# Layer 0's modulation in two halves, part of it multiplied on TensorE, and three half units ahead of it; products of a unit ordered by operand

## The reference

```python
c_act = jax.nn.silu(c)
for i in range(DEPTH):
    mod = c_act @ ada_w[i] + ada_b[i]
    sh1, sc1, g1, sh2, sc2, g2 = jnp.split(mod[:, None, :], 6, axis=-1)
    h = rms_norm(x, norm_mix[i]) * (1.0 + sc1) + sh1
    y = dilated_attention(h, ...)     # layer 0; hgrn2_mixer in layer 1
    x = x + g1 * y
    h = rms_norm(x, norm_ffn[i]) * (1.0 + sc2) + sh2
    x = x + g2 * swiglu(h, ffn_w1[i], ffn_w3[i], ffn_w2[i])
```

## Time and profile before

| | |
|---|---|
| median of 3 runs | 886.82 us (885.11 to 888.82) |
| the profiled execution's own time | 887.45 us |
| its span in the profile | 885.4 us |
| TensorE busy | 835.9 us, 94% of the span |
| VectorE busy | 613.0 us, 69% |
| ScalarE busy | 428.2 us, 48% |
| GpSimd busy | 125.0 us, 14% |
| data moved | 188.96 MB, mean 213 GB/s |

### The profile page before, as it was taken

One profiled execution on the slowest core, in us unless ns is written; L12 is line 12 of the kernel. 1 busy time (PEld: TensorE's weight loads), 2 busy tenths in 40 slices (PEclk: granted clock), 3 DMA queues, 4 the chain that ended last, 5 costly groups with the idle time before them and its releaser, 6 DMA issues.

```text
span 885.4 us, 10784 instructions
## 1 busy us (share of the span) xinstructions
PE 835.9 (94%) x4195; PEld 702.6 (79%) x4195; DVE 613.0 (69%) x736; ACT 428.2 (48%) x532; POOL 125.0 (14%) x160
## 2 busy tenths in 40 slices
PE   1599999999999989999999988999999899999998
PEld 0477888887888877888888877888888688888886
DVE  5979787788787856667756765787767665654554
ACT  3255454455455646344334355768475553433431
POOL 4101010101110100001010000376630000000000
PEclk9999999999999999999999999999999999999999
DMA  9899787877886823688787744443343477765621
GB/s 338 295 300 322 265 272 245 270 244 240 266 252 239 268 96 122 218 269 280 264 283 261 246 159 143 151 135 105 135 143 106 150 250 237 236 211 188 190 95 47
DMA packets 120039, 188.96 MB, mean 213 GB/s; under 512 B 5628, under 2 KB 91062, under 8 KB 119990
## 3 DMA queue, kind: packets, MB, share of 16 engines
q1 hardware_dynamic: 105782, 137.90, 48.2%
q0 software_dynamic: 14208, 50.39, 16.6%
HBM read 187.18 MB, written 1.09 MB: 213 GB/s over the span
## 4 chain that ended last, share of the span: by engine, by line
PE 85%; DVE 5%; DMA 3%; ACT 3%; issue 2%; SPq 2%; DVEq 0%; ACTq 0%
PE bank L454 71%; PE bank L756 3%; PE bank L588 2%; PE bank L563 2%; DMA raw<-in_attn_w_qkv_dram 1%; PE bank L544 1%; DVE acc L1198 1%; PE bank L509 1%; PE bank L707 1%; ACT arena L879 1%; DMA arena<-in_distance_table_dram 1%; DMA bias_rows<-arena 1%; SPq L303 1%; PE bank L506 1%; DVE acc L1193 1%
## 5 line engine op out<-in xcount | busy, mean ns | idle before, releaser
L1173 DVE TENSOR_TENSOR wlo<-raw,whi 128x2048 fp32r<-128x2048 f32 x123 | 285.4, 2324 | 50.8 <-ACT whi L830 50.7
L454 PE MATMUL bank<-whi,hT_hi 128*128 128x512 f32 (+1 forms) x776 | 305.1, 393 | 10.3 <-DVE hT_lo L1265 7.2
L454 PE MATMUL bank<-wlo,hT_hi 128*128 128x512 f32 (+1 forms) x800 | 306.2, 383 | 0.0
L454 PE MATMUL bank<-whi,hT_lo 128*128 128x512 f32 (+1 forms) x776 | 297.1, 383 | 0.0
L830 ACT ACTIVATE whi<-raw 128x2048 fp32r<-128x2048 f32 x123 | 235.4, 1916 | 34.2 <-DMA raw<-in_attn_w_qkv_dram 27.9
L454 PEld LDWEIGHTS bank<-whi,hT_hi 128*128 128x128 f32 x776 | 147.0, 189 | 41.2 <-DVE hT_lo L1265 9.4
L454 PEld LDWEIGHTS bank<-wlo,hT_hi 128*128 128x128 f32 x800 | 151.4, 189 | 29.1 <-issue 1.7
L454 PEld LDWEIGHTS bank<-whi,hT_lo 128*128 128x128 f32 x776 | 146.6, 189 | 28.9
L351 POOL DMA_DIRECT2D ada_w<-in_ada_w_dram x80 | 42.7, 534 | 523.9 <-DVE acc L1198 523.9
L1198 DVE SCALAR_TENSOR_TENSOR acc<-ada_w,cact,acc 128x1024 f32<-128x1024 f32 x80 | 102.3, 1279 | 3.0 <-DMA ada_w<-in_ada_w_dram 1.7
L454 PE MATMUL bank<-whi,oT_hi 128*128 128x512 f32 x240 | 97.2, 405 | 0.0
(11 more groups left out here) (146 smaller groups left out, 775.6 us busy)
## 6 DMA issues: line engine op xcount, KB each, us to landing
raw<-in_ffn_w_dram SPq DMA_DIRECT2D x88, 512.0 KB, 4.9
ada_w<-in_ada_w_dram POOLq DMA_DIRECT2D x80, 512.0 KB, 5.0
raw<-in_attn_w_qkv_dram SPq DMA_DIRECT2D x64, 512.0 KB, 5.7
raw<-in_ffn_w_dram SPq DMA_DIRECT2D x22, 1024.0 KB, 4.9
raw<-in_hgrn_w_in_dram SPq DMA_DIRECT2D x16, 1024.0 KB, 5.4
arena<-in_ada_w_dram POOLq DMA_DIRECT2D x16, 512.0 KB, 6.5
raw<-in_attn_w_qkv_dram SPq DMA_DIRECT2D x4, 1024.0 KB, 6.4
raw<-in_attn_w_out_dram SPq DMA_DIRECT2D x4, 1024.0 KB, 6.0
```

The costliest lines, as they stand in the source:

```text
L454: mm = nc.tensor.matmul(d[:, 0:n], l, r[:, k, cut], start=first and k == 0 and q == 0, stop=last and k == nk - 1 and q == 2)
L1173: nc.vector.tensor_tensor(wlo[:, m % RAW, :], raw[:, m % RAW, :], fp(hi_of(m)), ALU.subtract).then_inc(s["split"], 1)
```

## The change

The shift and the scale of layer 0 are worked out by halves instead of by blocks: half 0 is columns 0 to 511 of both shift and scale, half 1 the columns 512 to 1023 of both (`halves`). A chunk is still 128 rows and 512 KB, now in two pieces. Half 0 serves k-tiles 0 to 3, half 1 k-tiles 4 to 7.

- All these chunks, x, and the weight units go through SyncE's queue alone, in an order written out: c, chunks 0 and 1, x, chunks 2 to 7, unit 0 in four parts, chunk 8, unit 1, chunks 9 to 12, unit 2, chunks 13 to 15, then units from 3 on. The small rows, the relative bias and the distance table go through GpSimd's queue. The eight buffers are at other places, so that units can be loaded while they are in use.
- Of half 0's eight chunks VectorE adds up three (0, 2, 4); five (1, 3, 5, 6, 7: `ON_PE`) are multiplied by TensorE, eight one-column products each with the chunk as the stationary operand (`first_product`). Half 1 is all VectorE's (`first_sum`). The bias of the modulation comes in by its own rows.
- The raw transposed x is copied out of PSUM by ScalarE, and scale and shift are applied in place in SBUF.
- The order of the first head pair's units is changed (`ORDER0`): the three first are the upper halves (k-tiles 0 to 3) of chunks 0, 1 and 2, in three pairs of banks; units 3 to 5 are the lower halves. In these three (`first_half`) the products with `whi` come first for both tiles, then those with `wlo`.
- In every unit the products are ordered by operand: for a token tile all hi with whi, then all hi with wlo, then all lo with whi. The first waits for `rounded` and the hi part of the activation alone, `split` and the lo part are waited for where they are read.
- Later modulation blocks begin at unit 6 and take 8/5 products a unit in place of 11/8.

```diff
+ORDER0 = (0, 2, 4, 1, 3, 5, 6, 7, 8)
+ON_PE = (1, 3, 5, 6, 7)
...
+                j = ORDER0[j] if pr == 0 else j
...
-                if m == 0:
-                    sp.wait_ge(s["ada_used"], KC)
-                if PREFETCH <= m < RAW:
-                    sp.wait_ge(s["split"], m - PREFETCH + 1)
...
+            def first_load(n):
+                blk, k = divmod(n, KC)
+                if blk and k in ON_PE:
+                    sp.wait_ge(s["first_mm"], ON_PE.index(k) + 1)
+                elif blk:
+                    sp.wait_ge(s["first_sum"], first_sums(0, k) + 1)
+                sp.dma_start(first_w[k].rearrange("p (w c) -> p w c", w=2),
+                             halves(a["ada_w"][0, k * P:(k + 1) * P, :], blk)).then_inc(first_in[n], 16)
+            def load_unit(m):
                 if m >= RAW:
                     sp.wait_ge(s["pe_unit"], m - RAW + 1)
+                for src, nk, c0, n in pieces(m):
+                    slot = raw[:, m % RAW, :].rearrange("p (k n) -> p k n", k=nk)
+                    sp.dma_start(slot[:, :, c0:c0 + n], src).then_inc(raw_in[m % RAW], 16)
+            sp.dma_start(rows[0:KC, :], a["c"].rearrange("a (k d) -> (a k) d", d=P)).then_inc(s["c_in"], 16)
+            for n in range(2):
+                first_load(n)
+            sp.dma_start(x[:], a["x"][0].rearrange("(t p) d -> p t d", p=P)).then_inc(s["x_in"], 16)
+            for n in range(2, KC):
+                first_load(n)
+            for k in range(0, 4, 2):
+                for src, nk, c0, n in pieces(0):
+                    slot = raw[:, 0, :].rearrange("p (k n) -> p k n", k=nk)
+                    sp.dma_start(slot[:, k:k + 2, c0:c0 + n], src[:, k:k + 2, :]
+                                 ).then_inc(raw_in[0] if k else s["half_in"], 16)
+            first_load(KC)
+            load_unit(1)
+            for n in range(KC + 1, KC + 5):
+                first_load(n)
+            load_unit(2)
+            for n in range(KC + 5, 2 * KC):
+                first_load(n)
+            for m in range(3, UNITS):
...
+                if n == 2 * KC:
+                    pool.wait_ge(s["first_sum"], first_sums(1, KC))
                 if n >= 2 * KC + ADA_RING:
-                    pool.wait_ge(s["ada_used"], n - ADA_RING + 1)
+                    pool.wait_ge(s["ada_used"], n - 2 * KC - ADA_RING + 1)
...
+                def product(lhs, w, t, start, stop):
+                    for k in ks or range(nk):
+                        for c in cols or range(len(dst[t])):
+                            mm = nc.tensor.matmul(dst[t][c][:, 0:n], lhs[:, k0 + k, t * P:(t + 1) * P],
+                                                  w[:, k, c * 512:c * 512 + n],
+                                                  start=start and k == 0, stop=stop and k == nk - 1)
+                    return mm
+
+                pe.wait_ge(s["rounded"], m + 1)
+                for name, value in high:
+                    pe.wait_ge(s[name], value)
                 for t in tiles:
-                    for k in ks or range(nk):
-                        hi = lhs_hi[:, k0 + k, t * P:(t + 1) * P]
-                        lo = lhs_lo[:, k0 + k, t * P:(t + 1) * P]
-                        for c in cols or range(len(dst[t])):
-                            d = dst[t][c]
-                            cut = slice(c * 512, c * 512 + n)
-                            for q, (l, r) in enumerate(((hi, w[0]), (hi, w[1]), (lo, w[0]))):
-                                mm = nc.tensor.matmul(d[:, 0:n], l, r[:, k, cut],
-                                                      start=first and k == 0 and q == 0,
-                                                      stop=last and k == nk - 1 and q == 2)
+                    product(lhs_hi, w[0], t, first, False)
+                    if t == tiles[0]:
+                        pe.wait_ge(s["split"], m + 1)
+                    product(lhs_hi, w[1], t, False, False)
+                    if t == tiles[0]:
+                        for name, value in low:
+                            pe.wait_ge(s[name], value)
+                    mm = product(lhs_lo, w[0], t, False, last)
...
-                        pe.wait_ge(s["xn_lo"], 4 * q + 2 * t + j + 1)
-                        unit(m + j, hT_hi, hT_lo, 4, 4 * j, 512, dst, j == 0, j == 1, tiles=(t,))
-                    if q == 0:
-                        continue
+                        n = 4 * q + 2 * t + j + 1
+                        unit(m + j, hT_hi, hT_lo, 4, 4 * j, 512, dst, j == 0, j == 1, tiles=(t,),
+                             high=[("xn_hi", n)], low=[("xn_lo", n)])
...
+            def first_product(k):
+                pe.wait_ge(first_in[k], 16)
+                slot = ON_PE.index(k)
+                for j in range(KC):
+                    mm = nc.tensor.matmul(bank[3][:, slot * KC + j:slot * KC + j + 1], first_w[k][:, j * P:(j + 1) * P],
+                                          cact[:, k:k + 1], start=True, stop=True)
+                mm.then_inc(s["first_mm"], 1)
+            def first_reduce(half, dst):
+                pe.wait_ge(s["first_sum"], first_sums(half, KC))
+                for j in range(KC):
+                    mm = nc.tensor.matmul(dst[:, j:j + 1], acc[:, half, j * P:(j + 1) * P], ones[:, 0:1],
+                                          start=True, stop=True)
+                mm.then_inc(s["mod_red"], 1)
+            pe.wait_ge(s["c_in"], 16)
             pe.wait_ge(s["pool_setup"], 5)
-            nc.tensor.transpose(bank[0][:, 0:NROWS], rows[0:NROWS, :], ident[0:NROWS, 0:NROWS]).then_inc(s["cols_t"], 1)
+            nc.tensor.transpose(bank[0][:, 0:KC], rows[0:KC, :], ident[0:KC, 0:KC]).then_inc(s["c_t"], 1)
+            pe.wait_ge(s["cact_s"], 1)
+            first_product(1)
+            first_product(3)
+            pe.wait_ge(s["rows_in"], 16 * (len(ROWS) + 1))
+            nc.tensor.transpose(bank[1][:, 0:NROWS], rows[0:NROWS, :], ident[0:NROWS, 0:NROWS]).then_inc(s["cols_t"], 1)
+            norm_t(0, 0)
+            first_product(5)
+            norm_t(0, 1)
             pe.wait_ge(s["rel_in"], 16 * 5)
-            nc.tensor.matmul(bank[1][0:GH, 0:TABLE], rel3, tabw, start=True, stop=True).then_inc(s["tab_mm"], 1)
-            for t in range(T):
-                norm_t(0, t)
-            for r in range(3):
-                reduce_task(r, 3 if r < 2 else 2)
+            nc.tensor.matmul(bank[2][0:GH, 0:TABLE], rel3, tabw, start=True, stop=True).then_inc(s["tab_mm"], 1)
+            first_reduce(0, bank[3][:, len(ON_PE) * KC:(len(ON_PE) + 1) * KC])
+            first_product(6)
+            first_product(7)
...
+            def first_half(m):
...
+                if m == 0:
+                    pe.wait_ge(s["half_rounded"], 1)
+                    pe.wait_ge(s["xn_hi"], 1)
+                    product(hT_hi, w[0], 0, True, False, ks=(0, 1))
+                    pe.wait_ge(s["rounded"], 1)
+                    product(hT_hi, w[0], 0, False, False, ks=(2, 3))
+                else:
+                    pe.wait_ge(s["rounded"], m + 1)
+                    product(hT_hi, w[0], 0, True, False)
+                pe.wait_ge(s["xn_lo"], 1)
+                product(hT_lo, w[0], 0, False, False)
+                pe.wait_ge(s["xn_hi"], 2)
+                product(hT_hi, w[0], 1, True, False)
+                pe.wait_ge(s["xn_lo"], 2)
+                product(hT_lo, w[0], 1, False, False)
+                if m == 2:
+                    first_reduce(1, bank[7])
+                pe.wait_ge(s["split"], m + 1)
+                product(hT_hi, w[1], 0, False, False)
+                product(hT_hi, w[1], 1, False, False).then_inc(s["pe_unit"], 1)
+            first_half(0)
             pe.wait_ge(s["tab_cp"], 1)
+            pe.wait_ge(s["mod_sum"], 1)
+            first_half(1)
+            pe.wait_ge(s["h0_raw"], 4)
+            first_half(2)
...
+            def first_modulation(half):
+                dve.wait_ge(s["mod_red"], half + 1)
+                src = bank[7][:, 0:KC]
+                if half == 0:
+                    dve.wait_ge(s["first_mm"], len(ON_PE))
+                    src = small[:, 48:56]
+                    n = (len(ON_PE) + 1) * KC
+                    nc.vector.tensor_reduce(src, bank[3][:, 0:n].rearrange("p (s j) -> p j s", j=KC), AX_X, ALU.add
+                                            ).then_inc(s["mod_sum"], 1)
+                    dve.wait_ge(s["mod_sum"], 1)
+                at = 48 if half else 56
+                b = cols[:, BIAS0:BIAS0 + 2 * KC].rearrange("p (w h c) -> p w h c", w=2, h=2)[:, :, half, :]
+                v = lambda y: y.rearrange("p (w c) -> p w c", w=2)
+                nc.vector.tensor_tensor(v(small[:, at:at + KC]), v(src), b, ALU.add).then_inc(s["mod_sum"], 1)
+                dve.wait_ge(s["mod_sum"], half + 2)
+                scale_gain(0, 0, small[:, at + 4:at + 8], 4 * half, 4).then_inc(s["mod_ev"], 1)
+                dve.wait_ge(s["mod_ev"], half + 1)
...
+            first_sum(0, 4)
```

(25 more changed lines are left out.)

363 lines of the change are left out of this document (204 added, 159 removed).

## The result

| | before | changed |
|---|---|---|
| median of 20 runs | 887.88 us (884.07 to 891.51) | 890.17 us (884.68 to 893.52) |
| ratio | | 1.0027, 95% interval 1.0014 to 1.0039 |
| the profiled execution's time, span | 887.45, 885.4 | 889.58, 887.8 |

The changed kernel is 2.3 us slower. That is less than 0.5%, yet the interval leaves no doubt of the sign. The forecast was 883.0 with a range up to 888: the time lies 2.2 us above the range.

A forecast was written before the change was run, and what follows sets the result against it. TensorE, busy for 94% of the span, was taken to bound the kernel. Terms -0.6 - 3.6 + 0.4 = -3.8 gave 883.65 against 887.45, or 883.0 against the median; own range 880.5 to 886, full range 874 to 888.

The forecast's parts named there:

- the list of the start: TensorE's unbroken work from chunk 3 at about 12.0 to 34.9, 3.5 us a chunk product, first unit matmul at 37.0.
- The rival of the rising clock: Clock rises during the start's list: it ends near 25.5, time 871.7, or 877.8 if only after the table; chance 0.20.
- Only unit matmuls bring the fast level: At the start, other TensorE work stays slow, 0.22 us a pass, twice the later 0.11.
- pays for the slow level as before: Unit 0: nine matmuls in some 3.9 us, fifteen at 0.228, done at 44.4.
- The sum over half 1: TensorE's sum over the partitions after sixteen matmuls of unit 2: 1.7 us at the fast level, ending at 55.2.
- split 3: VectorE's split for unit 3, 2.2 us, behind half 1's second lo part, ending at 61.3.
- I take half of it, 0.8: Unit 3's 3 us pause may cost the fast level for a stretch, 1.7 lost; half taken, unit 6 at 79.3.
- 0.6 gained: Net gain at unit 6: 80.36 before, 79.3 forecast, less 0.44 for transposes still to do.
- 0.4 lost: Later modulation products moved behind unit 5: a 0.64 wait goes at unit 11, units 20 and 29 lose 0.5 each.
- five starts of sub-layers: First matmul no longer waits for half a lo part: 5 x 0.72, 3.6 us gained.
- the rival that the order gives nothing: The order in a unit gives nothing and the start may lose its gain: 887; chance 0.12.
- The rival that came out slower: Later products fall behind their loads, 1 us late in nine units beyond VectorE's slack: 892; chance 0.10.

The follow-up runs named there:

- run 4: The changed kernel with GpSimd's memset of 1024 columns of `acc` cut into eight pieces; 887.2 us, ratio 0.9995 to the kernel before.
- Run 6: The changed kernel with VectorE's split of unit 3 moved ahead of half 1's two lo parts; 885.68 us, ratio 0.9994 to the kernel before.
- run 10: The changed kernel with two chunks on TensorE, unit 3 split early, clearing in eight pieces, plus unread 128-column matmuls in TensorE's start pauses; 875.25 us, ratio 0.9865.
- Run 8: The kernel before with a unit's products ordered by operand and GpSimd's clearing in eight pieces; 884.97 us, ratio 0.9974.
- Run 9: The changed kernel with two chunks on TensorE, unit 3 split early, clearing in eight pieces, later products spread 14 to nine units; 877.73 us, ratio 0.989.
- run 3: The changed kernel with one later modulation product in units 2, 4 and 6 of a head pair, two in all others; 889.68 us, ratio 1.0038.
- Run 1: The changed kernel with each unit's products k by k again behind all their waits; 894.14 us, ratio 1.0082 to the kernel before.
- run 2: The kernel before with only the new order of products and later wait for the lo part; 885.93 us, ratio 0.9992.
- run 5: The changed kernel with two chunks (1 and 3) on TensorE and the other six on VectorE; 878.68 us, ratio 0.9904 to the kernel before.

## Why the prediction was wrong, step by step

**Right: the list of the start.** Each product 3.4 to 3.6 us (said 3.5), the end at 34.3 (34.9), the first unit matmul at 36.96 (37.0), VectorE idle for 16.8 us (17), and the slow level all through. The rival of the rising clock was wrong for this execution, but not for all: it rose late in the list in the profiled executions of runs 4 and 6, some 3 us worth. (Its 25.5 halves everything behind product 3, the transposes of the rows and of x too; from product 5 on alone the list would end near 26.6.) "Only unit matmuls bring the fast level" held for the trace before and not in run 10, where product 1 took 1.85 us behind matmuls of 128 columns.

**Wrong by 0.8: unit 0 "pays for the slow level as before", done at 44.4.** It was done at 45.2; not nine but some thirteen of its matmuls were slow, 0.43 us each. (The 0.38 that the prediction read is too small: 3.4 us for nine counts two that lie partly outside the window; from 41.36 to 45.30 the nine took 3.94. The sum used 3.9 and is not touched.) The sum over half 1 therefore ended at 56.1, not 55.2, and split 3 at 62.5, not 61.3; the chain between them took 6.3 us (said 6.1).

**Wrong by 0.9: "I take half of it, 0.8".** The fall of the clock came whole: the four groups of four matmuls from 62.51 take 5.36 us, start to start, where four at the full level take 3.63, so 1.7 us. With the 1.2 above that puts unit 6 at 81.4; it was 81.55. Here the whole 0.6 gained turned into 1.6 lost. Run 6 shows that the pause and the fall were both the price of one place in VectorE's order: with split 3 first, the pause is 0.52 and nothing falls.

**Wrong by 3.2, the step that failed most: "0.4 lost" for the later products.** It was 3.65. Of the 6.2 us between the forecast and the measured sum, this term has 3.2, the way to unit 6 has 2.2 and the starts of sub-layers 0.7. Two parts of it failed. I counted units 20 and 29 as those with two products ahead of a normalisation in place of one; by the rule they are 15, 20, 24 and 29, and all four have a new wait: 0.13, 0.53, 1.28 and 1.67 us. (The wait of 0.64 us did shrink, to 0.21.) And I priced a product from VectorE's time alone. In units 24 and 29 GpSimd clears `acc` in the moment in which VectorE needs 0.16 us for eight columns; 0.98 us of each of these two waits goes with the clearing in pieces (run 4). The kernel before has one such meeting, in unit 22, behind its wait of 1.47 us, one of the three in the earlier trace rows, which I had counted without asking what ended it; the changed kernel loses that one (0.51 is left) and gains two. Run 8 shows it in the kernel before. Run 9 shows the part of the products: with never two of them ahead of a normalisation, no wait for q and k is left. But there, as in run 3, the time went elsewhere: no version here has both short waits and products that find their loads.

**Right in kind, a bit too large: five starts of sub-layers.** Each wait fell from 1.45 to 0.81, 0.65 instead of 0.72, so 3.2 of the 3.6; 2.9 are left at the end. Run 1 confirms it in the changed kernel, where the rival that the order gives nothing falls. In the kernel before, run 2 shows the waits shorter but little in the medians.

**The rival that came out slower had its place nearly right and its price wrong.** Products wait for their loads five times, 6.8 us, in place of three times, 1.7. Little of it reached TensorE there: only one wait, 0.31 us ahead of output transposes, stands behind such a load. It became real in runs 3, 9 and 10, where the products were bunched or the rest had become faster.

**Not asked at all: whether five chunks on TensorE were too many.** The forecast noted that VectorE would be idle for 17 us and TensorE busy all the while, and took that as given. Three chunks back to VectorE were worth 10.9 us (run 5), more than everything forecast for the change. The forecast had both costs, and did not compare the 3.5 us that a chunk costs TensorE with the 1.2 it costs an idle VectorE.

## What to carry to other kernels

Work moved to the bounding engine to fill its pause pays only as far as it is the cheaper place: a chunk cost TensorE 3.5 us here and VectorE 1.3, and the work is better divided so that both end together. Look at every wait of the kernel before that the change will pass again, and at what the engines next to the named one did in that microsecond; a 0.16 us operation that lasted 1.20 was a collision here, and it came back in two other units when the change moved the two together. A pause of 3 us on TensorE had a price in the clock behind it, here 1.7 us more.
